# Hybrid attention and recurrence block: distance of tokens and weights, 512-column row units, attention's products

## The reference

```python
# first block, 272 tokens
a = rms_norm(h, norm_mix)
(q_na, k_na, v_na, q_hg, z_f, z_b, i_hg, g_hg, gate_na, gate_hg) = split_cols(a @ w_in)
y_na = neighbourhood_attention(q_na, k_na, v_na, rpb) @ w_na_out     # 8 heads of 64
y_hg = hgrn2_branch(q_hg, z_f, z_b, i_hg, g_hg, lb, hg_norm) @ w_hg_out
h = h + (sigmoid(gate_na) * y_na + sigmoid(gate_hg) * y_hg) @ w_o
h = h + square(relu(rms_norm(h, norm_mlp) @ w_up)) @ w_down
x = rms_norm(h, norm_final)[:, 16:]
# second block, 256 tokens, each layer with adaLN shift, scale and gate = silu(c) @ ada_w + ada_b
# even layer: a, u, v, gate = split(h @ even_in); pool mixer(a), spatial gating(u, v); @ even_out
# odd layer:  gla (4 heads) and stick-breaking attention (8 heads of 128) of h @ odd_in; @ odd_out
return rmsnorm(x, final_g)
```

## Time and profile before

| | |
|---|---|
| median of three runs | 891.46 us (891.33 to 893.07) |
| profiled execution | 892.68 us, span 890.9 us |
| PE, PEld busy | 857.3 us, 828.8 us |
| DVE, ACT, POOL busy | 638.0, 495.2, 95.9 us |
| mean granted clock of TensorE | 0.99 |
| HBM read | 166.60 MB, 188 GB/s over the span |

### The profile page before, as it was taken

The page is one execution under the profiler, slowest core; times in us unless marked ns, Lnnn a source line. Parts: engine busy times, 40 slices in busy tenths (PEclk is TensorE's granted clock), DMA queues, the critical chain, the costliest instruction groups (busy, mean ns, idle before and its releaser), DMA issues.

```text
span 890.9 us, 17086 instructions
## 1 busy us (share of the span) xinstructions
PE 857.3 (96%) x6910; PEld 828.8 (93%) x6910; DVE 638.0 (72%) x1066; ACT 495.2 (56%) x910; POOL 95.9 (11%) x113
## 2 busy tenths in 40 slices
PE   5988999999999999999999989999999999999996
PEld 5976879998999999999999989999999999999995
DVE  5844755995599776868688886776888549576663
ACT  6534445765555746464666663554577457556541
POOL 0000007530102000000030430000202030000001
PEclk9989999999999999999999999999999999999999
DMA  9721343345358896979767745555656336765431
GB/s 363 244 76 48 95 142 116 116 147 159 101 172 275 290 350 238 338 248 334 243 201 244 233 170 166 189 182 198 183 163 189 106 100 212 257 219 179 146 97 48
DMA packets 46989, 168.75 MB, mean 189 GB/s; under 512 B 5168, under 2 KB 6320, under 8 KB 46784
## 3 DMA queue, kind: packets, MB, share of 16 engines
q1 hardware_dynamic: 46448, 165.08, 56.2%
q10 hardware_dynamic: 464, 2.59, 0.8%
HBM read 166.60 MB, written 1.05 MB: 188 GB/s over the span
## 4 chain that ended last, share of the span: by engine, by line
PE 87%; DVE 7%; ACT 2%; issue 2%; DMA 1%; SPq 0%; POOL 0%; DVEq 0%; ACTq 0%
PE bank L183 86%; DVE wl L222 2%; DMA raw<-in_ws 1%; DVE raw L210 1%; PE bank L186 1%; DVE h L210 1%; SPq L180 0%; ACT L198 0%; DVE A L210 0%; DVE B0l L222 0%; DVE B1l L210 0%; ACT wh L192 0%; ACT th L189 0%; DVE nm L216 0%; DVE sP L222 0%
## 5 line engine op out<-in xcount | busy, mean ns | idle before, releaser
L222 DVE TENSOR_TENSOR wl<-raw,wh 128x1024 fp32r<-128x1024 f32 x259 | 323.3, 1262 | 17.6 <-ACT wh L192 16.8
L192 ACT CAST wh<-raw 128x1024 fp32r<-128x1024 f32 x259 | 268.7, 1047 | 106.9 <-PE bank L183 78.2
L183 PE MATMUL bank<-XAh,wl 128*128 128x256 f32 (+1 forms) x896 | 258.7, 289 | 3.0 <-ACT vM L192 2.0
L183 PE MATMUL bank<-XAh,wh 128*128 128x256 f32 (+1 forms) x896 | 251.9, 281 | 0.0
L183 PE MATMUL bank<-XAl,wh 128*128 128x256 f32 (+1 forms) x896 | 251.6, 281 | 0.0
L183 PEld LDWEIGHTS bank<-XAh,wl 128*128 128x128 f32 x896 | 170.0, 190 | 7.4 <-issue 3.2
L183 PEld LDWEIGHTS bank<-XAh,wh 128*128 128x128 f32 x896 | 170.1, 190 | 0.1
L183 PEld LDWEIGHTS bank<-XAl,wh 128*128 128x128 f32 x896 | 169.9, 190 | 0.0
L183 PE MATMUL bank<-B1h,wl 128*128 128x256 f32 (+1 forms) x464 | 131.4, 283 | 1.5 <-DVE B1l L210 1.5
L183 PE MATMUL bank<-B1h,wh 128*128 128x256 f32 (+1 forms) x464 | 130.3, 281 | 0.0
L183 PE MATMUL bank<-B1l,wh 128*128 128x256 f32 (+1 forms) x464 | 130.2, 281 | 0.0
(11 more groups left out here) (247 smaller groups left out, 1301.1 us busy)
## 6 DMA issues: line engine op xcount, KB each, us to landing
raw<-in_ws SPq DMA_DIRECT2D x307, 512.0 KB, 4.3
bias<-in_bias ACTq DMA_DIRECT2D x1, 1536.0 KB, 9.5
h<-in_xt SPq DMA_DIRECT2D x4, 272.0 KB, 5.0
out<-h SPq DMA_DIRECT2D x4, 256.0 KB, 2.4
C<-in_cst SPq DMA_DIRECT2D x1, 800.0 KB, 8.1
crow<-in_crow ACTq DMA_DIRECT2D x1, 512.0 KB, 12.8
wT<-in_wt SPq DMA_DIRECT2D x1, 512.0 KB, 5.9
bS<-in_bs SPq DMA_DIRECT2D x1, 512.0 KB, 6.8
```

Source lines behind the costliest of these rows:

```text
L183: return self.real.matmul(*a, **k)
L192: return self.real.copy(*a, **k)
L222: return self.real.tensor_tensor(*a, **k)
```

## The change

1. **Addresses.** Slots of `wh` and `wl` are 1056 columns apart, and `half` shifts the 1024 columns that are used by 32 columns (128 bytes), depending on the slot's number and on whether the unit is streamed. XA and XU have 320 columns a k. B0 and B1 have 256 columns a k, and only the stages `a`, `glr` and `qk`, whose operand has 258 columns, see them with 264 (F0, F1). All stages that stream 256 tokens of XA use its columns 16 to 271. `wh` still begins at 128 modulo 256, XA and XU at 0 and 64, B0 and B1 at 64. For that, `anew` and `gw` move into `crow` by a later DMA (`late`, 512 KB), and the table C shrinks by 256 KB.
2. **Row stages.** v, i, vn and gv take units of two k-steps by 512 columns; sv keeps 256. One matmul streams 512 columns into a whole bank. The number of units stays.
3. **Attention.** `norm`'s reciprocal (`share`) stays on VectorE, ahead of the score instead of behind it; the product goes to GpSimd. Two heads share an output bank, so the copy to B0h and the subtraction to B0l are done for two heads at once. The steps per unit are 2, 3, 3, 2 for v, zf, zb, qh.
4. **adaLN items** stand at other places of the plan: 43 behind units 58 to 121 and 5 behind units 123 to 135 (before: 36, 4 behind 137 to 143, and 8 behind 221 to 235).

VectorE's order in the attention, before: one QK step with bias for head s, and the next (`wl` is the split of a weight unit, `nm` the maximum, sum and reciprocal).

The core of the diff:

```diff
-                out.append(("m", name, k, 4, c, w))
+            for k in range(k0, k0 + nk, 1024 // w):
+                out.append(("m", name, k, 1024 // w, c, w))
 
     mat("w_in", 512, 1024)
     mat("w_in", 0, 512)
-    mat("w_in", 1024, 1536)
+    mat("w_in", 1024, 1536, w=512)
     mat("w_in", 2048, 2560)
     mat("w_in", 2560, 3072)
     mat("w_in", 1536, 2048)
-    mat("w_in", 3072, 3584)
+    mat("w_in", 3072, 3584, w=512)
     mat("w_in", 3584, 6144)
     mat("w_na_out", 0, 1024, nk=4)
     mat("w_hg_out", 0, 1024, nk=4)
@@ -64,7 +64,7 @@
         mat("w_down", 0, 1024, k0=8 * g)
     first = len(out)
     mat("even_in", 0, 1024)
-    mat("even_in", 2048, 3072)
+    mat("even_in", 2048, 3072, w=512)
     mat("even_in", 3072, 4096)
...
-        if ada and (58 <= n < 122 and n % 9 % 2 == 0 or 136 <= n < 144 and n % 2 or n >= 220 and n % 2):
+        if ada and (58 <= n < 122 and n % 9 in (0, 2, 3, 4, 6, 8) or 122 <= n < 144 and n % 3 == 0):
...
-        for col in range(c0, c1, 256):
+        width = min(512, c1 - c0)
+        kn = 1024 // width
+        for col in range(c0, c1, width):
             start(col - c0)
-            for q in (0, 4):
+            for q in range(0, 8, kn):
                 j = self.unit_of[name, q, col]
                 self.feed(j)
-                unit(j, q, 4, col - c0)
+                unit(j, q, kn, width, col - c0)
                 self.between()
-                if q == 0:
+                if q + kn < 8:
                     self.step()
             self.step()
             leave(col - c0)
...
+        wh = sbt(ctx, "wh", [128, NSPLIT, 1056], F32R)
+        hp = sbt(ctx, "hp", [128, 28])
+        wl = sbt(ctx, "wl", [128, NSPLIT, 1056], F32R)
+        XAh = sbt(ctx, "XAh", [128, 8, 320], F32R)
+        XAl = sbt(ctx, "XAl", [128, 8, 320], F32R)
+        rsB = sbt(ctx, "rsB", [128, 272])
+        B0s = [sbt(ctx, f"B0{n}", [128, 2112], F32R) for n in "hl"]
...
+        def in_rows(x, n):
+            return x[:, 0:8 * n].rearrange("p (k n) -> p k n", n=n)
+
+
+        B0h, B0l, B1h, B1l = (in_rows(x, 256) for x in (*B0s, *B1s))
+        F0h, F0l, F1h, F1l = (in_rows(x, 264) for x in (*B0s, *B1s))
+        B0, B1, F0, F1 = (B0h, B0l), (B1h, B1l), (F0h, F0l), (F1h, F1l)
+        XA = (XAh[:, :, 16:272], XAl[:, :, 16:272])
...
+        def streams(j):
+
+            _, name, _, _, col, _ = items[mats[j]]
+            return any(name == n and c0 <= col < c1 for n, c0, c1 in (
+                ("w_in", 1024, 1536), ("w_in", 3072, 3584), ("even_in", 2048, 3072), ("odd_in", 1024, 2048),
+                ("odd_in", 4112, 5136)))
+
         def half(j):
-            return wh[:, j % NSPLIT, :], wl[:, j % NSPLIT, :]
+            n = j % NSPLIT
+            o = 32 if n % 2 != streams(j) else 0
+            return wh[:, n, o:o + 1024], wl[:, n, o:o + 1024]
 
...
+                        if i - NRAW == last_ada:
+                            e.dma_start(crow[:, :], late).then_inc(one["late"], 16)
...
-                        o = ps[po:po + 64, 0:256]
+                        if hh % 2 == 0:
+                            side.take("pv", hh // 2)
+                        o = bk("pv", hh // 2)[po:po + 64, 0:256]
                         e.wait_ge(*at("turned", (hh, 1)))
-                        e.wait_ge(*at("v", (256 * (hh // 4), 2)))
+                        e.wait_ge(*at("v", (0, 2)))
                         for r in range(2):
                             e.matmul(o, vN[:, r, 64 * hh:64 * hh + 64], PT[hh % 2][:, r, :], start=r == 0, stop=False)
                         e.matmul(o, vM[:, 64 * hh:64 * hh + 64], PTm[hh % 2][:, :], start=False,
                                  stop=True).then_inc(*up("pv", hh))
-                        if hh:
-                            side.give(("pv", hh - 1), ("na_high", hh - 1), ("na_low", hh - 1))
+                        if hh % 2:
+                            side.give(("pv", hh // 2), ("na_high", hh // 2), ("na_low", hh // 2))
                         yield
-                side.give(("pv", 7), ("na_high", 7), ("na_low", 7))
 
             w.side.append(attention())
+            w.steps = 2
+            t_rows("v", "w_in", 1024, 1536, XM, X_of("mix"), lambda b, col: [("v", (col, b))], (0, 16, 144))
             w.steps = 3
-            t_rows("v", "w_in", 1024, 1536, X, X_of("mix"), lambda b, col: [("v", (col, b))], (0, 16, 144))
-            t_tiles("zf", "w_in", 2048, 2560, X, X_of("mix"), lambda t: [("tanh", ("zf", t))], n1=272)
+            t_tiles("zf", "w_in", 2048, 2560, XM, X_of("mix"), lambda t: [("tanh", ("zf", t))], n1=272)
+            t_tiles("zb", "w_in", 2560, 3072, X, X_of("mix"), lambda t: [("tanh", ("zb", t))])
             w.steps = 2
-            t_tiles("zb", "w_in", 2560, 3072, X, X_of("mix"), lambda t: [("tanh", ("zb", t))], n0=16, n1=272)
-            t_tiles("qh", "w_in", 1536, 2048, X, X_of("mix"), lambda t: [("silu", ("qh", t))], n0=16, n1=272)
+            t_tiles("qh", "w_in", 1536, 2048, X, X_of("mix"), lambda t: [("silu", ("qh", t))])
             w.drain()
 
...
                     if s >= 2:
-                        hh = s - 2
-                        po = 64 * (hh % 2)
-                        e.wait_ge(*at("pv", hh))
-                        e.copy(B0h[po:po + 64, hh // 2, 0:256], bk("pv", hh)[po:po + 64, 0:256]).then_inc(
-                            *up("na_high", hh))
+                        if s % 2:
+                            p = s // 2 - 1
+                            e.wait_ge(*at("pv", s - 2))
+                            e.copy(B0h[:, p, :], bk("pv", p)[:, 0:256]).then_inc(*up("na_high", p))
                         yield
...
-                def norm(hh, t):
-                    S, nm = sP[(2 * hh + t) % 4], nmr[(2 * hh + t) % 4]
+                def share(hh, t):
+                    nm = nmr[(2 * hh + t) % 4]
                     e.wait_ge(*at("exp", (hh, t)))
                     e.reciprocal(nm[:, 2:3], nm[:, 1:2]).then_inc(*up("share", (hh, t)))
-                    e.wait_ge(*now("share"))
-                    e.tensor_scalar(S[:, :], S[:, :], nm[:, 2:3], None, ALU.mult).then_inc(*up("prob", (hh, t)))
-
-                def na_low(hh):
-                    po = 64 * (hh % 2)
-                    low((B0h[po:po + 64, hh // 2, 0:256], B0l[po:po + 64, hh // 2, 0:256]),
-                        bk("pv", hh)[po:po + 64, 0:256], ("na_high", hh), "na_low", hh)
+
+                def na_low(p):
+                    low((B0h[:, p, :], B0l[:, p, :]), bk("pv", p)[:, 0:256], ("na_high", p), "na_low", p)
...
+                            if s > 0:
+                                share(s - 1, t)
...
-                            if s > 0:
-                                norm(s - 1, t)
                             yield
                     if s == 8:
-                        norm(7, 0)
-                        norm(7, 1)
+                        share(7, 0)
+                        share(7, 1)
                     if 1 <= s <= 8:
                         for t in range(2):
                             yield
                     if s >= 2:
-                        if s >= 3:
-                            na_low(s - 3)
                         yield
-                na_low(7)
+                        if s % 2:
+                            na_low(s // 2 - 1)
 
             w.side.append(attention())
-            w.steps = 3
+            w.steps = 2
...
+            def attention():
+                def norm(hh, t):
+                    S, nm = sP[(2 * hh + t) % 4], nmr[(2 * hh + t) % 4]
+                    e.wait_ge(*at("share", (hh, t)))
+                    e.tensor_scalar(S[:, :], S[:, :], nm[:, 2:3], None, ALU.mult).then_inc(*up("prob", (hh, t)))
+
+                for s in range(10):
+                    if s < 8:
+                        for t in range(2):
+                            if s > 0:
+                                norm(s - 1, t)
+                            yield
+                    if s == 8:
+                        norm(7, 0)
+                        norm(7, 1)
+                    if 1 <= s <= 8:
+                        for t in range(2):
+                            yield
+                    if s >= 2:
+                        yield
+
+            w.side.append(attention())
```

149 lines of the change are left out of this document (72 added, 77 removed).

## The result

The changed kernel takes 880.44 us (median of 4 runs, 878.87 to 881.22) against 891.42 us before (891.33 to 893.07), a ratio of 0.987 with a 95% interval of 0.9853 to 0.9888. It is faster, by 11 us where 29 were forecast: 880.4 instead of 862.5 us, above the range of 854 to 877.

A forecast was written before the change was run, and what follows sets the result against it. TensorE, busy 96% of the span, was taken as the bound, mostly through the interval between matmuls. Terms 15.1 + 4.3 − 1.0 + 11.5 − 1.3 + 0.3 = 28.9 us off 892.68 gave 863.8, as median 862.5 us; range 854 to 877.

The forecast's parts named there:

- parts 2 to 4: The forecast's terms besides distance: row stages by 512 columns, attention and adaLN products; 13.8 us gained by the rest.
- Distance: Part 1, tile and row stages: 4182 chain matmuls go from 117.6 to 114.0 ns at distance 192; 15.1 us (9.6 to 17.6).
- The k = 3 of the earlier trace: In down1 before the change, the block at distance 192 took 0.69 us against 0.71, read as an effect of distance.
- rule of two independent read ports: Rival for all TensorE streams: distance is worth nothing, so 877.6 us without the 15.1; chance 7%.
- The slower rival: Rival for matmuls at 192: one constant distance locks streams in a bad phase at 125 ns, 31 us lost, 909 us; 3%.
- Rows by 512: Part 2, i, vn and gv: 528 matmuls of 256 columns become 264 of 512 at 220 ns; 4.3 us (0.4 to 6.2).
- The end of vn: Part 2, at 527 us: last copies and squares come in one 512-column piece, SGU norm ready about 1 us later; −1.0 us.
- Attention: Part 3, 96.31 us stretch: transposes nearly stop waiting, low clock mostly goes, GpSimd's product 0.8 us; 11.5 us (4 to 16).
- adaLN: Part 4: one new product where the chain runs through VectorE in o and up0, a takes one more; −1.3 us.
- Start: Kernel start: later load of `late` and the smaller table C; +0.3 us.
- what would show it: Signs: 0.68 us blocks for every k in down1 and eo0, up0 to down3 5 us shorter, attention 85 us, vn near 21.2.
- stay three: Sign against the forecast, in attention: low-clock pieces remain three, where at most one piece at 0.50 was expected.

The follow-up runs named there:

- oldpitch: The changed kernel with the old pitches of weight and token tiles, so the distance changes from matmul to matmul again: 892.16 us, ratio 1.0002.
- again: The changed kernel run and profiled once more, unchanged (the repeat): 879.67 us (876.07 to 887.52), the slowest run being the profiled one.
- kick: The changed kernel with 16 matmuls cut into 16 and 240 columns near the starts of stretches: 878.06 us, ratio 0.9839.
- d64: The changed kernel with the 32-column shift on the other half of the weight slots, so all 256- and 512-column matmuls stand at distance 64: 885.75 us, ratio 0.9929.
- kickvn: kick with vn and gv in units of 256 columns and one cut in each: 877.8 us, in two groups of runs.
- rows256: The changed kernel with its row stages (v, i, vn, gv) in units of 256 columns again, at distance 192: 886.24 us (882.18 to 890.19).
- attdve: kick with attention's product with the reciprocal back on VectorE, right behind the reciprocal, instead of GpSimd: 880.91 us.
- kickada: kick with adaLN operations moved out of o, up0, down3 and a; four in vn, ten over u to eo1: 877.94 us.
- micro: Model left out, only 256- to 512-column matmul streams between stops: of 12 tile streams at distance 192, 8 at 113.3 and 4 at 117.8 ns.
- micro2: Model left out, 89 streams with repeated starts at each distance, some with kicks: 11 of 12 starts at 192 fast, 4 of 12 at 64, none at 160.

## Why the prediction was wrong

The direction was right; the sum was 18 us too large. By oldpitch 3.3 us of that, or some 2 more against the addresses of before, are the distance, forecast as one price for every matmul. The larger share is in parts 2 to 4, forecast at 13.8 us together and worth next to nothing: the attention's gain was less than half of the forecast, and what vn's 512 columns bring was more than lost in ga. Step by step:

- **Distance, 15.1 us forecast.** "192 is the good distance and needs a few matmuls to settle" was half of it. Settled streams are better than the 114.0 that I took (113.3), but at one constant distance they also have a second steady interval, 117.8, which is about the mean of before (117.6). While the distance changed every few matmuls no stream stayed in either. The step that failed here is the assumption of one price for all 4182 matmuls: in the first profile u to eo1, some 800 of them, got nothing (2.9 us of the sum), and in the repeat up1 to down3 got nothing either (158.29 against 158.06 before). Shown by the stream alone, by again and by kick. What the distance gave in all is shown by oldpitch: 11.8 us of 15.1 by the medians, 1 to 2 less against the addresses of before. The k = 3 of the earlier trace rows was the right reading; only that several streams at 192 were followed for a few matmuls each hid the second state. The Trainium skill's rule of two independent read ports ("TensorE: Matmul & The Clock Gate", "Step-by-step: what each phase is for") was rightly set aside: oldpitch and d64 change nothing but addresses and differ by 12 and 5 us from the changed kernel.
- **The slower rival, 3%.** Its mechanism is the one that occurred: one distance locks a stream in a bad phase. Its price was wrong: the bad phase is 117.8 ns, not 125, so it takes the gain away and adds nothing. That the time still came out lower is partly luck: how many stretches stood at 113.3 was not forecast, and the same kernel ran from 876.1 to 887.5 us.
- **Rows by 512, 4.3 us forecast.** vn gained 0.29, gv 0.33, i 0.24 us. The price of 220 ns failed; measured 233.3 (range named: 213 to 235). I took the excess over 106.7 ns for each 256 columns as 7 ns once per instruction; at 192 it is 6.6 ns for 256 columns and 20 for 512, and 13 at the best distance for 512. And at 192 the 512-column matmul has its worst value: 226.7 at 0, 228.9 at 64.
- **The end of vn, -1.0 forecast.** ga lost 2.3 us in the first profile and 3.8 in kick. Part 2 was forecast at +3.3 with this term and came out negative: the change's own 0.3 us in vn costs 2 to 5 in ga. kickvn against kick shows it (27.58 and 32.56 us; one has no piece at the low clock, the other 6.8 us, which is some 3.4 of the 5.0), and rows256 against the repeat of the changed kernel at equal clock (29.05 and 30.82).
- **Attention, 11.5 us forecast, 5.1 measured, 2.1 in the repeat.** This is the largest miss. The step that failed is that the transposes would no longer wait: their waits were to fall from 4.7 us to 0.5, and they are 4.0. GpSimd's product takes 0.96 us, not 0.8, alone and beside a score. Once, at 117.8 us, it took 1.92 beside a VectorE split, and a transpose waited 2.5 us for it:

```profile
59.28 0.96 POOL L219 TENSOR_SCALAR sP<-sP,nm 128x272 f32<-128x272 f32 x1 [5.05 <-DVE nm L207]
117.78 2.86 POOL L219 TENSOR_SCALAR sP<-sP,nm 128x272 f32<-128x272 f32 x2 [6.43 <-DVE nm L207]
```

  (The second line is two products, 1.92 and 0.96 us.) I counted the product as hidden behind the score; attdve shows that it was not (2.7 us). The stop for vM came as forecast, 3.0 us of waiting and 3.4 from start to start, with a 3.4 us piece at the low clock behind it. A second piece came at 120 us behind the wait for that transpose, and in the repeat there were three, 13.6 us in all: that the low clock would mostly go (5.3 us of the forecast, 1.5 back) failed with the waits.
- **adaLN, -1.3 forecast.** o +0.4, up0 -0.8 and a +1.4, a loss of 1.0 in all (with what the distance gave up0 in it): the sum was nearly right, the place was not, since "takes one more" was read from a's 21.43 of 24.39 us of VectorE, an average over the stage. In kickada up0 loses 1.5 and a 1.4 us without them. How much a loses follows the stretch ahead of it: 25.8 us in the four profiles with this plan in which up1 to down3 ran at 113.3 ns, 24.8 to 24.9 in the six in which it ran at 117.8 or 118.2. A faster stretch leaves VectorE, 125.5 us busy in it, less time to be ahead; that reason is argued, the two groups are in the traces.
- **Start, +0.3 forecast.** k began 0.6 us and the attention 0.5 us earlier. Tenths.

That oldpitch ends at before's time while attention is 4.9 us shorter means that parts 2 to 4 together were worth nothing against its addresses, 1 to 2 us against those of before, not 14. Of "what would show it", blocks of 0.68 us for every k held in down1 and failed in eo0, and up0 to down3 came out 6.5 us shorter (5 were named); "every 230 ns or more" was named as what would prove the rows wrong, and did. Low-clock pieces that "stay three" was another such sign: the attention has two in the first profile and three in the repeat.

What stays open: what in a stop decides the phase in which a stream starts (equal stops gave both), and why the low clock falls on other places from run to run with the same waits.

## What to carry to other kernels

When an interval between matmuls depends on addresses, measure a long stream at each candidate with many starts before pricing it: the mean of short mixed runs hides that a constant distance can have more than one steady state. Part of the gain on the bound engine is then a matter of chance until something sets the state, so profile the same kernel more than once and compare stages, not totals. And a stage's last unit should be small where the next one waits for its result: halving the instructions in vn cost more behind it than it saved. Moving work off a busy engine helps only if the new engine's own duration fits into the wait: here GpSimd's 0.96 us stood where VectorE's 0.36 had stood.

## What the runs showed of the hardware

- A stream of fp32r matmuls of 256 columns at distance 192 (moving less stationary address, modulo 256 bytes) runs at 113.3 or 117.8 ns and can keep it for over 150 us (again, the changed kernel); at 64 the same two, mostly the slow one; at 0 and 96 120, at 160 117.3 to 120 ns (micro, micro2).
- A matmul cut in two (16+240 columns) costs 0.12 us once. In the kernels' profiles it freed a slow stream at 192 when it stood one ahead of the longest of three, left it when it stood at it, and moved the phase by one when it stood behind it. At 64 it freed none of 16. Three matmuls at distance 160 freed 4 of 4 streams for 0.02 us; a wait on a semaphore that had come changed none of 4 streams (one of them slow).
- A 512-column matmul takes 226.7, 228.9 (once 233.3) and 233.3 ns at distances 0, 64 and 192: the order of the distances is not that of 256 columns.
- A GpSimd product with a per-partition scalar on 272 columns took 0.96 us alone or beside a VectorE operation that reads the score's bank, and 1.92 us the one time that a VectorE subtraction of 1024 columns had begun 0.12 us before it; VectorE's own took 0.36.
- The low clock comes and goes with the same waits: the changed kernel's attention had 6.8 us of it in one profile and 13.6 in the other, for 3.0 us.
